# Loading x by quarters of its columns, with the first weights between, and taking its squares behind the column tiles

## The reference

```python
def rmsnorm(x, g, eps=NORM_EPS):
    xf = x.astype(jnp.float32)
    y = xf * lax.rsqrt(jnp.mean(xf * xf, axis=-1, keepdims=True) + eps)
    return (y * g.astype(jnp.float32)).astype(x.dtype)

h = rmsnorm(x, norm_mix_g[i])
u = h @ w_in[i]
```

## Time and profile before

| | us |
|---|---|
| median of 3 runs | 1907.5 |
| lowest and highest | 1907.28, 1909.22 |
| profiled execution | 1908.02 |
| its span in the trace | 1906.2 |

### The profile page before, as it was taken

One profiled execution on the slowest core, in us unless ns is written; L12 is line 12 of the kernel. 1 busy time (PEld: TensorE's weight loads), 2 busy tenths in 40 slices (PEclk: granted clock), 3 DMA queues, 4 the chain that ended last, 5 costly groups with the idle time before them and its releaser, 6 DMA issues.

```text
span 1906.2 us, 23419 instructions
## 1 busy us (share of the span) xinstructions
PE 1876.2 (98%) x9426; PEld 1546.0 (81%) x9426; DVE 1081.1 (57%) x1713; ACT 853.9 (45%) x1318; POOL 177.0 (9%) x217
## 2 busy tenths in 40 slices
PE   7999999999999999999999999999999999999997
PEld 5887778878788888887878888898888888888876
DVE  5779565447445656688734335423345446656675
ACT  6435553333344444556634323433233444444563
POOL 2110121102010201100100000000000010201100
PEclk9999999999999999999999999999999999999999
DMA  6233311128564747532431222232355354747531
GB/s 226 69 83 124 92 56 40 45 67 308 157 141 135 174 139 165 156 72 81 143 122 44 89 67 89 89 99 90 100 189 190 96 132 133 177 137 159 158 88 66
DMA packets 175581, 228.20 MB, mean 120 GB/s; under 512 B 15849, under 2 KB 119955, under 8 KB 175474
## 3 DMA queue, kind: packets, MB, share of 16 engines
q1 hardware_dynamic: 151954, 181.91, 29.4%
q0 software_dynamic: 21936, 42.49, 12.0%
q10 hardware_dynamic: 1584, 2.30, 0.3%
HBM read 212.96 MB, written 15.54 MB: 120 GB/s over the span
## 4 chain that ended last, share of the span: by engine, by line
PE 90%; DVE 4%; ACT 2%; DMA 2%; issue 1%; SPq 0%; POOLq 0%; ACTq 0%; DVEq 0%
PE bank L131 88%; PE bank L134 2%; DVE wl L155 1%; DMA raw<-in_w_in_dram 1%; ACT L141 1%; ACT wh L141 1%; DVE XL L163 1%; DVE T L155 0%; DMA RB<-in_w_ff_dram 0%; DMA xs<-in_x_dram 0%; DVE ACC L155 0%; ACT GP L141 0%; DVE xt L163 0%; DVE XT L155 0%; ACT T L141 0%
## 5 line engine op out<-in xcount | busy, mean ns | idle before, releaser
L131 PE MATMUL bank<-XH,wh 128*128 128x512 f32 (+1 forms) x1272 | 505.6, 398 | 5.1 <-DVE XL L163 2.2
L131 PE MATMUL bank<-XL,wh 128*128 128x512 f32 (+1 forms) x1272 | 498.2, 392 | 2.6 <-DVE XL L163 2.6
L141 ACT ACTIVATE wh<-raw 128x1024 fp32r<-128x1024 f32 (+1 forms) x239 | 252.4, 1057 | 519.9 <-PE bank L131 515.6
L155 DVE TENSOR_TENSOR wl<-raw,wh 128x1024 fp32r<-128x1024 f32 x238 | 292.6, 1230 | 294.9 <-ACT wh L141 294.5
L131 PE MATMUL bank<-XH,wl 128*128 128x512 f32 x1264 | 317.2, 392 | 0.0
L131 PEld LDWEIGHTS bank<-XH,wh 128*128 128x128 f32 (+1 forms) x1272 | 239.6, 188 | 60.8 <-issue 3.5
L131 PEld LDWEIGHTS bank<-XL,wh 128*128 128x128 f32 (+1 forms) x1272 | 239.8, 189 | 52.8 <-DVE XL L163 4.0
L131 PEld LDWEIGHTS bank<-XH,wl 128*128 128x128 f32 x1264 | 235.4, 188 | 49.3 <-issue 0.6
L155 DVE TENSOR_TENSOR wl<-RB,wh 128x1024 fp32r<-128x1024 f32 x112 | 136.7, 1224 | 91.3 <-ACT wh L141 91.1
L141 ACT ACTIVATE wh<-RB 128x1024 fp32r<-128x1024 f32 x112 | 118.5, 1061 | 141.8 <-PE bank L131 128.7
L131 PE MATMUL bank<-wl,SH 128*128 128x512 f32 x448 | 138.2, 390 | 1.2 <-DVE wl L155 1.1
(11 more groups left out here) (447 smaller groups left out, 2634.7 us busy)
## 6 DMA issues: line engine op xcount, KB each, us to landing
raw<-in_w_in_dram SPq DMA_DIRECT2D x58, 1024.0 KB, 5.2
RB<-in_w_ff_dram SPq DMA_DIRECT2D x16, 1024.0 KB, 5.1
raw<-in_w_ff_dram SPq DMA_DIRECT2D x16, 1024.0 KB, 5.7
RB<-in_w_ff_dram POOLq DMA_DIRECT2D x32, 512.0 KB, 7.7
RB<-in_w_mlp_dram SPq DMA_DIRECT2D x16, 1024.0 KB, 5.0
raw<-in_w_mlp_dram SPq DMA_DIRECT2D x16, 1024.0 KB, 5.3
RB<-in_w_mlp_dram POOLq DMA_DIRECT2D x32, 512.0 KB, 8.0
raw<-in_w_out_dram SPq DMA_DIRECT2D x8, 1024.0 KB, 6.2
```

The costliest lines, as they stand in the source:

```text
L131: return self.put(ns, lambda e: e.matmul(out, lhsT, rhs, start=start, stop=stop, skip_group_check=True))
L141: return self.put(ns, lambda e: e.activation(out, in_, func, bias=bias, scale=scale), func)
L155: return self.put(self.ns(out), lambda e: e.tensor_tensor(out, a, b, op))
```

## The change

x is one tile of 128 x 4 x 1024 instead of four tiles. It is loaded in four quarters of 256 columns, each with the rows of all 512 tokens (row pieces of 1 KB instead of 4 KB), and each quarter completes two column tiles. Behind the first and second quarter SP issues the two halves of weight chunk 0, which before came behind all of x; `sp_w` leaves that chunk out. TensorE transposes tile by tile: for each f the four token blocks. The four squares wait for all of x and for XH of tile 7; before, the first three waited only for their block of x and the fourth for XH of tile 3 as well. The amounts of bytes, matmuls, transposes and squares stay as they are.

```diff
@@ sp_w
+            if ci == 0:
+                continue
             raw = c["raw"]
             src = c["w"][128 * c["k0"]:128 * (c["k0"] + nk), c["c0"]:c["c0"] + ncol].rearrange("(k p) n -> p k n", p=128)
-            if ci == 0:
-                sp.dma_start(raw[:, :, 0:128], src[:, :, 0:128]).then_inc(*self.sig("rawa").up16(("first", 0)))
-                sp.dma_start(raw[:, :, 128:256], src[:, :, 128:256]).then_inc(*self.sig("rawb").up16(("first", 1)))
-            else:
-                sp.dma_start(raw, src).then_inc(*self.sig(f"raw{ci % NRAW}").up16(("chunk", ci)))
+            sp.dma_start(raw, src).then_inc(*self.sig(f"raw{ci % NRAW}").up16(("chunk", ci)))
@@ begin_tiles
-        self.xs = [self.m("xs", 2 * j, [128, 1024]) for j in range(4)]
+        self.xs = self.m("xs", 0, [128, 4, 1024])
@@ sp_begin
-        x = a["x"][0].rearrange("(j p) d -> j p d", p=128)
-        for j in range(4):
-            yield
-            sp.dma_start(self.xs[j][:, :], x[j]).then_inc(*self.sig(f"x{j}").up16(("xs", j)))
+        x = a["x"][0].rearrange("(j p) d -> p j d", p=128)
+
+        for c in range(4):
+            cs = slice(256 * c, 256 * c + 256)
+            yield
+            sp.dma_start(self.xs[:, :, cs], x[:, :, cs]).then_inc(*self.sig(f"x{c}").up16(("xs", c)))
+            if c < 2:
+                ch = self.chunks[0]
+                src = ch["w"][0:1024, ch["c0"]:ch["c0"] + 256].rearrange("(k p) n -> p k n", p=128)
+                half = slice(128 * c, 128 * c + 128)
+                sp.dma_start(ch["raw"][:, :, half], src[:, :, half]).then_inc(*self.sig(f"raw{'ab'[c]}").up16(("first", c)))
@@ pe_begin
-        for j in range(4):
-            for f in range(8):
-                yield
-                pe.wait_ge(self.at("xs", j))
-                if f == 7:
-                    pe.wait_ge(self.at("g0"))
-                i = pe.transpose(self.ps[f][:, 128 * j:128 * j + 128], self.xs[j][:, 128 * f:128 * f + 128], self.ident[:, :])
-                if j == 3:
-                    i.then_inc(*s.up(("xT", f)))
+        for f in range(8):
+            yield
+            pe.wait_ge(self.at("xs", f // 2))
+            if f == 7:
+                pe.wait_ge(self.at("g0"))
+            for j in range(4):
+                i = pe.transpose(self.ps[f][:, 128 * j:128 * j + 128], self.xs[:, j, 128 * f:128 * f + 128], self.ident[:, :])
+            i.then_inc(*s.up(("xT", f)))
@@ ac_begin
-            ac.wait_ge(self.at("xs", j), *([self.at("h", "X0", 3)] if j == 3 else []))
-            ac.activation(self.junk[:, j, :], self.xs[j][:, :], ACT.Square, accum=self.ss[:, j:j + 1]).then_inc(*s.up(("ss",)))
+            ac.wait_ge(*[self.at("xs", c) for c in range(4)], self.at("h", "X0", 7))
+            ac.activation(self.junk[:, j, :], self.xs[:, j, :], ACT.Square, accum=self.ss[:, j:j + 1]).then_inc(*s.up(("ss",)))
```

## The result

The changed kernel takes 1910.85 us in the median of 22 runs (1908.77 to 1912.74), the one before 1907.52 in as many. The ratio is 1.0016, with a 95% interval of 1.0009 to 1.0022: 3.3 us slower, beyond the interval, and within the 0.2% that the prediction called no change. Forecast were 1903.2 us and a range up to 1908.5. The two profiled executions (1909.3 and 1908.0) lie 1.5 under and 0.5 above the medians of their kernels, so this pair of traces shows 1.3 of the 3.3 us.

A forecast was written before the change was run, and what follows sets the result against it. TensorE, busy for 98% of the span, bounds the kernel, so only an earlier start or less waiting pays. -3.3 and -1.0 make -4.3 us: 1908.0 - 0.5 - 4.3 = 1903.2 us, range 1899.5 to 1908.5.

The forecast's parts named there:

- The loads: Start, loads of x: third quarter lands at 12.0 us, last at 13.4, chunk's first half 6.4, second quarter 7.9, second half 9.6.
- The price taken for shorter rows: Loads of x: 0.31 us for 512 B rows plus 0.33 for 1 KB rows, up to the third quarter's landing.
- TensorE's first part: Start of the dense matmul stream: the run from rw 13 on starts at 15.0 instead of 18.30, -3.3 us.
- the clock's term: Half-rate stretch on rw 13's 12 matmuls, 1.7 us lost before: taken as unchanged, 0, bounds -1.7 to +1.7 us.
- Squares and RST: ScalarE's later squares: T ready at 22.6 and hidden, RST in time; price 0, ends 0 and +1.8 us.
- Later loads: Third chunk issued earlier, landing well before 30 us, so TensorE's wait on LD goes: -1.0 us, ends -1.1 and 0.
- The sum: Whole kernel: -3.3 and -1.0 make -4.3 us, giving 1903.2 us; the forecast's own range is 1901.5 to 1905.
- The 1.5 us either way for a new order: Rest of the kernel: the planner's new order may swap near-equal steps anywhere, allowed for with 1.5 us either way.
- the two slower forms: Before rw 13: T's transposes stand ahead, 1911.8, chance 0.08; or XT of tile 1 behind the squares, 1909.5, chance 0.06.
- the third case: Start: third quarter lands at 12.7, LD stays late as ScalarE is full; most gain missing, centre 1906, chance 0.26.
- The slower rival: TensorE's order: T's transposes ahead of rw 13's matmuls, waiting from 15.0 until 22.6; +4.3 us, 1911.8, chance 0.08.
- The forecast that a planner places steps by readiness: TensorE's order: the planner moves T's transposes with the squares, held against the form at 1911.8, chance 0.08.

## Why the prediction was wrong

- **The loads.** x's third quarter landed at 3.2 + 9.1 = 12.3 (12.0 forecast), the last at 13.8 (13.4), the chunk's first half at 6.6 (6.4). The second quarter landed at 8.9 and the second half at 10.7, each a microsecond after the forecast. The price taken for shorter rows, 0.64 us, was right in sign and short of the 0.85 measured: the 323 GB/s taken for 512 B rows come from a stretch that mixes them with rows of 1 KB. The Trainium skill (DMA: Bandwidth & Descriptors, Specifications), by which both row lengths run at line rate, would have given 11.45; the trace has 12.3.
- **TensorE's first part, -3.3.** The total is right in this pair of traces, by luck; the way to it isn't. rw 13's first matmul came at 16.73, not 15.0: the planner had put the transposes of tiles 4 to 7 in one block behind eight matmuls, which ended 1.3 us after the third quarter had landed. These started 0.43 us apart up to 12.83, and the eight transposes at 8.93 took as long as the 16 at 13.58: the pace of the 1.2 GHz level. (The profile gives a granted clock of 1.00 there, but the trace's first record of the clock is at 12.9 us.) At 0.23 us apart they would have ended about 1.2 us earlier, with the quarter's landing. The 12 matmuls of rw 13 then took 2.8 us instead of 4.44. -1.6 and -1.7 make the 3.25 us by which 19.49 is earlier than 22.74. So the clock's term, which I had at 0 for want of a row, was -1.7 against before's profile; but that 1.7 is a cost of one execution of before, which the other four traces with its loads don't have. Against those the quarters give about 2 us, not 3.3.
- **Squares and RST, 0.** T was ready at 24.3 (22.6 forecast; its spreading queued behind wl of unit 2 on VectorE) and its transposes, at the end of the pair as forecast, were not waited for, with 0.6 us of cover instead of 2. The failing step is the next one. I listed what is queued behind the squares on ScalarE, the XT copies and wh of unit 2, and stopped there. RST's own copy is on that queue too; I had worked out when RST is needed, but not when its copy gets its turn, and priced it at 0. The change moved both estimates: by the program's own model (its `arrange`, run on both kernels) RST is copied at 25.3 instead of 22.7, and the third chunk lands at 23.5 instead of 24.3. wh of unit 4 so came ahead of RST, and RST took on that chunk's landing: it was copied at 32.63, and TensorE, whom the ring of three banks carried to 31.1, stood for 2.9 us.
- **Later loads, -1.0 for LD; "it still lands well before 30".** It landed at 31.6. I had put the 13.2 us of the earlier trace rows down to the spills and to volume, and the queue ahead of it to eight small loads. The runs show four of these, with one row of 256 B for all partitions, to hold the queue. The trace of before had a sign of it, if a mixed one: a stretch at a quarter of the usual rate while the chunk was outstanding (97 GB/s from 18 to 22 us; with lambda's own rows still only 172). I counted bytes, where a hole in the DMA row should have been asked for its cause. So the wait on LD didn't go; it became a wait on T of 2.9 us and 3 us of half rate.
- **The sum.** By unit 3 the stream's lead was 3.1 us (31.12 against 34.22). -3.1, less the 4.84 us that before took from unit 3's start to LD, plus 2.94 of stop and 6.64 for unit 3's high parts, is 40.70 - 39.06 = +1.6 in this execution, +1.3 in the span. I took no account of a stop's second price, the clock. The 1.5 us either way for a new order weren't needed: from 46 us on the order is that of before. (The waits of before from 45 us on are nine groups and 8.0 us, two of 0.2 more than the prediction read; nothing hangs on them.)
- **The rivals.** In number the two slower forms came nearest (1911.8 and 1909.5, chances 0.08 and 0.06), by luck: neither TensorE's place for T's transposes nor XT of tile 1 held anything. In mechanism the third case came nearest, most of the gain gone and LD late because ScalarE is full, with its centre at 1906. It had the place right, ScalarE's queue from 18 us on, but not what it waits for, and it ended 5 us short. The slower rival had T's transposes in a bad place on TensorE; the misplaced step was the copy behind them, on ScalarE. The forecast that a planner places steps by readiness was no argument: it places by its estimate, and for one load this estimate, 23.5 against a landing at 31.6, was 8 us off.

What stays open: why executions of one kernel differ in their half-rate stretches, and so how the median's 3.3 us divide into stop and clock. The two profiles of the changed kernel have spans 1.3 and 3.0 us above before's, and before's has 1.7 us of half rate on rw 13 that may make the difference look smaller; how often an execution of before has them isn't known from one profile. How the reads of one row slow the engines wasn't looked into.

## What to carry to other kernels

When an edit lets one engine run earlier, ask of each in-order queue which step now stands in front of the critical one, and what it waits for; an order made by a model is only as good as its worst estimate of a landing. A hole in the DMA row while a load is outstanding is a finding, not slack. And a stop of the matmul stream has a second price, the clock behind it: here stops of 2.9, 3.8 and 5.0 us each cost about 3 us more. Last, before one trace is compared with one trace, look at where each has its half-rate stretches: here one of them made up half of an apparent lead.

## What the runs showed of the hardware that was not expected

- Four loads in which all 128 partitions read one row of 256 B hold their queue: with them ahead a load of 1 MiB landed 15.8 to 18.7 us after its issue at 14 to 15 us, with 128 own rows each 11.4, moved away 11.0. In the slow stretch 95 GB/s flowed with the DMA engines busy for 0.39, against 383. The same with one row of 2 KB showed no effect (11.3). With before's loads, where the chunk is issued at 19 to 20 us, the four loads ahead of it gave 13.2 in one trace and 6.3 in another, against 6.1 with own rows.
- After stops of 2.7, 2.9, 3.8, 5.0 and 6.9 us TensorE's granted clock was at 0.50 for several us; after stops of 1.1, 1.4 and 1.6 us it was not.
- The same loads and the same first matmuls met the half rate at different places: at 18.4 us in the one trace of before, near 14 us in three others, not at all up to 36 us in a fifth. Near 905 us it lasted longer in six of the 14 traces (mean granted clock 0.83 from 895 to 925 us, against 0.89 in the others), and these six lost 0.6 to 1.2 us against before there.
